# Latent projections of a two-block transformer kernel: from one full-precision product to three rounded ones with ring weights

## What is computed

```python
q = (_rmsnorm(c_q, q_a_g) @ w_uq).reshape(b, n, A_HEADS, A_QK)       # 256 -> 8 * 96
kv = (_rmsnorm(c_kv, kv_a_g) @ w_ukv).reshape(b, n, A_HEADS, A_NOPE + A_V)  # 128 -> 8 * 128
k_nope, v = kv[..., :A_NOPE], kv[..., A_NOPE:]
q, k = _rmsnorm(q, q_norm_g), _rmsnorm(k, k_norm_g)                  # then rope, then attention
```

## Time and profile before

| what | value |
|---|---|
| runs of the kernel before | 891.93 us (891.77 to 892.02) |
| the profiled execution's own time | 892.2 us |
| its span, first to last instruction | 890.4 us |
| PE / PE weight load / DVE / ACT busy | 869.1 / 711.8 / 627.2 / 440.3 us |
| DMA | 136.68 MB, 154 GB/s in the mean |
| granted PE clock, mean | 0.995 of full |

### The profile page before, as it was taken

The page is one execution under the profiler, slowest core; times in us unless marked ns, Lnnn a source line. Parts: engine busy times, 40 slices in busy tenths (PEclk is TensorE's granted clock), DMA queues, the critical chain, the costliest instruction groups (busy, mean ns, idle before and its releaser), DMA issues.

```text
span 890.4 us, 13376 instructions
## 1 busy us (share of the span) xinstructions
PE 869.1 (98%) x5372; PEld 711.8 (80%) x5372; DVE 627.2 (70%) x1252; ACT 440.3 (49%) x750; POOL 21.2 (2%) x16
## 2 busy tenths in 40 slices
PE   7999999999999999999999999999999999999996
PEld 4678477777687777877998888988999888888885
DVE  4532857585826769966699999978588775565666
ACT  3351516544623355655543454466555665555552
POOL 0000000000000000000002212000000000000000
PEclk9999999999999999999999999999999999999998
DMA  9794551100354034303556656441365365545541
GB/s 348 289 329 161 213 189 60 48 25 1 119 220 141 13 130 142 99 10 142 168 190 189 188 186 193 142 144 60 106 200 205 118 204 199 197 172 198 188 167 47
DMA packets 39997, 136.68 MB, mean 154 GB/s; under 512 B 4352, under 2 KB 4480, under 8 KB 39680
## 3 DMA queue, kind: packets, MB, share of 16 engines
q1 hardware_dynamic: 38928, 130.48, 42.9%
q10 hardware_dynamic: 1008, 5.36, 1.6%
HBM read 134.77 MB, written 1.05 MB: 153 GB/s over the span
## 4 chain that ended last, share of the span: by engine, by line
PE 72%; DVE 21%; ACT 3%; DMA 2%; issue 1%; SPq 1%; DVEq 0%; ACTq 0%
PE ps L417 8%; PE ps L973 6%; DVE wlo L1474 5%; PE ps L372 4%; PE ps L373 4%; PE ps L418 4%; DVE AF L1943 4%; PE ps L377 4%; PE ps L735 3%; PE ps L491 2%; PE ps L400 2%; DMA AF<-wmod 2%; PE ps L389 2%; PE ps L462 2%; PE ps L758 2%; PE ps L401 2%
## 5 line engine op out<-in xcount | busy, mean ns | idle before, releaser
L1474 DVE TENSOR_TENSOR wlo<-raw,whi 128x1024 fp32r<-128x1024 f32 (+2 forms) x204 | 231.7, 1158 | 33.4 <-ACT whi L1011 33.2
L1011 ACT ACTIVATE whi<-raw 128x1024 fp32r<-128x1024 f32 (+2 forms) x204 | 203.6, 1005 | 86.5 <-DMA raw<-wpack 45.2
L372 PE MATMUL ps<-hx,whi 128*128 128x256 f32 (+1 forms) x384 | 115.3, 300 | 0.3 <-ACT AF L1352 0.3
L417 PE MATMUL ps<-hx,whi 128*128 128x512 f32 x320 | 113.9, 398 | 0.0
L373 PE MATMUL ps<-hx,whi 128*128 128x256 f32 (+1 forms) x384 | 112.0, 292 | 0.0
L377 PE MATMUL ps<-hx,wlo 128*128 128x256 f32 (+1 forms) x332 | 96.9, 292 | 0.0
L418 PE MATMUL ps<-hx,wlo 128*128 128x256 f32 x320 | 89.8, 281 | 0.0
L372 PEld LDWEIGHTS ps<-hx,whi 128*128 128x128 f32 x384 | 73.4, 191 | 3.8 <-issue 2.3
L373 PEld LDWEIGHTS ps<-hx,whi 128*128 128x128 f32 x384 | 73.5, 191 | 2.0 <-issue 0.7
L462 PE MATMUL ps<-whi,hx 128*128 128x512 f32 (+1 forms) x192 | 71.7, 373 | 0.5 <-ACT acc L1080 0.5
L417 PEld LDWEIGHTS ps<-hx,whi 128*128 128x128 f32 x320 | 60.1, 188 | 14.6
(11 more groups left out here) (293 smaller groups left out, 1666.7 us busy)
## 6 DMA issues: line engine op xcount, KB each, us to landing
raw<-wpack SPq DMA_DIRECT2D x178, 512.0 KB, 4.2
AF<-wmod SPq DMA_DIRECT2D x48, 512.0 KB, 6.1
raw<-wpack SPq DMA_DIRECT2D x24, 256.0 KB, 3.7
XT<-xin SPq DMA_DIRECT2D x4, 512.0 KB, 6.3
raw<-wpack SPq DMA_DIRECT2D x4, 432.0 KB, 4.7
uq<-wuq ACTq DMA_DIRECT2D x2, 768.0 KB, 5.8
cst<-cpack ACTq DMA_DIRECT2D x1, 1093.0 KB, 8.1
AF<-wukv ACTq DMA_DIRECT2D x2, 512.0 KB, 7.1
```

Of the source, the lines that this page charges most:

```text
L372: e.matmul(o, wh[:, b], xh(k), start=j == 0, stop=False, skip_group_check=True)
L417: e.matmul(ps.ap(key, 512).rearrange("p (s n) -> p s n", s=2), wh[:, b], K.hx[:, :, k, 0:256], start=k == 0, stop=False, skip_group_check= ...
L1011: e.activation(W.hi(i), W.raw(i), ACT.Copy).then_inc(*HI.up(j))
L1474: e.tensor_tensor(W.lo(i), W.raw(i), W.hi(i), ALU.subtract).then_inc(*LO.up(j))
```

## The change

The latents are kept as a rounded half and a rest, and `w_uq` and `w_ukv` become chunks in the ring. `kv_proj` and `q_proj` make three fp32r matmuls where they made one f32 matmul. ACT writes the rounded latents where it wrote the plain ones; DVE makes the rests, reading PSUM, ahead of the lows of the `gvkr` chunks, and the banks are free only after that. The `uq` and `wkv` loads leave ACT's queue. In layer 0 `w_ukv` and `w_uq` each pass the ring twice (once for each pair of token tiles), in layer 1 once: three chunks of 1024 and six of 768 columns more, in the order gvkr, ukv, uq, uq, fmix, fgate. The calls of `highs` and `lows` for `gvkr` look one chunk ahead in layer 1 too, and new calls take `uq` (behind the tables) and `ukv` for the second pair. SP's groups of chunks between the modulation pieces are shifted by the new chunks.

```diff
-        def kv_proj(p):
-            pe.wait_ge(K.ukv_in["ukv", l], A[l, "ckv"])
+        def kv_proj(*ps_):
+            c, wh, wl = weights((l, "ukv", ps_[0]), ("w_ukv", l, (0,), ("kvc", 1024)), 1024)
...
+                        pe.wait_ge(A[l, "ckv"], *ps.take((l, nm, t)))
+                        e.matmul(o, K.ckvh[:, x], wh[:, b], start=True, stop=False, skip_group_check=True)
+                        e.matmul(o, K.ckvh[:, x], wl[:, b], start=False, stop=False, skip_group_check=True)
+                        pe.wait_ge(V[l, "ckvl"])
+                        e.matmul(o, K.ckvl[:, x], wh[:, b], start=False, stop=True, skip_group_check=True).then_inc(*M.up((l, nm, t)))
+        def q_proj(p):
+            got = [weights((l, "uq", p, m), ("w_uq", l, (m,), (0, 768)), 768) for m in range(2)]
...
-        kv_proj(0)
         if l == 0:
+            kv_proj(0)
             q_proj(0)
...
-            kv_proj(1)
+            kv_proj(0, 1)
             q_proj(1)
@@ scalar_program @@
-            ps.give(key, A.now())
...
-        e.dma_start(K.uq[:, :], K.wuq[l]).then_inc(*K.uq_in.up(("uq", l)))
-        e.dma_start(g.wkv, K.wukv[l]).then_inc(*K.ukv_in.up(("ukv", l)))
...
         for i in range(3):
-            highs((l, "gvkr", "w", i), NHL - 1 if l else 1)
+            highs((l, "gvkr", "w", i), 1)
+        highs((l, "uq", l, 1), 0)
...
+            highs((l, "ukv", 1), 0)
@@ vector_program @@
+        dv.wait_ge(K.c1["cst"], *bar)
+        for m in range(2):
+            key = (l, "cq", m)
+            dv.wait_ge(A[key])
+            e.scalar_tensor_tensor(out=g.cql[:, m, :], in0=ps.ap(key, N), scalar=C("qag", 2 * l + m, 1), in1=g.cqh[:, m, :], op0=ALU.mult, op1=ALU.subtract).then_inc(*V.up((l, "cql", m)))
+            ps.give(key, A[l, "cqsq", m], V.now())
+        key = (l, "ckv", 0)
+        dv.wait_ge(A[l, "ckv"])
+        e.scalar_tensor_tensor(out=K.ckvl, in0=ps.ap(key), scalar=C("kvag", l, 1), in1=K.ckvh, op0=ALU.mult, op1=ALU.subtract).then_inc(*V.up((l, "ckvl")))
+        ps.give(key, A[l, "ckvsq"], V.now())
         for i in range(3):
-            lows((l, "gvkr", "w", i), NHL - 2 if l else 1)
+            lows((l, "gvkr", "w", i), 1)
...
         V.mark((l, "tab"))
+        lows((l, "uq", l, 1), 0)
         bias(l, 4)
...
             bias(1, 0)
+            lows((l, "ukv", 1), 0)
             kv_take(1, 0, M[l, "kT", 0, 1, 4])
@@ sync_program @@
-    chunks(15, 17)
+    chunks(15, 20)
     mods(2)
-    chunks(17, 18)
+    chunks(20, 21)
     mods(3)
-    chunks(18, 19)
+    chunks(21, 22)
     mods(4)
     mods(5)
     at_out = W.of[0, "wout", 7] + 1
-    chunks(19, at_out)
+    chunks(22, at_out)
```

## The result

The changed kernel takes **918.6 us** in the median of four runs (916.3 to 923.1), the kernel before 891.9 beside it (891.8 to 892.0): 1.031 times the time, with an interval of 1.028 to 1.033. That is 2.6 us over the 916.0 of the forecast and inside its range. The profiled execution took 917.0, its span is 915.2 us. The runs after spread over 7 us, those of before over 0.3.

What follows compares the result with a forecast made beforehand. The order written into the queues, not engine load, was taken to decide, with PE busy 869 of 890 us. A 5.9 + 1.7, kv_proj(1) -0.7, B 4.7 + 0.8, C 10.2 + 1.7 gave +24.3, so 916, range 905 to 923.

Steps and rivals of the forecast that it cites:

- The products: K, V and query projections: 0.68 us per K or V product, 2.1 for 2.6 per query tile; 5.8 less PE work.
- A: Layer 0, fgate 1: its low is made behind the vf copies, so PE starts 5.9 us late, plus 1.7 clock.
- B: Layer 0 loop, step 9: ACT waits for wout 0's load behind gu 0's low; +4.7 us, plus 0.8 clock.
- C: Layer 1: gvkr's banks free 2.7 us late, fgate 0's low behind the normalisations; +10.2 us in all, plus 1.7 clock.
- The loads: Two loads a layer move from ACT's to SP's queue, where waits in order ahead of a load can delay it.
- The clock: Lower clock behind PE's long rests: 1.7 us each at fgate 1 and layer 1's fgate 0, half at step 9.
- The sum: Whole kernel: waits and clock losses less kv_proj(1)'s 0.7 make +24.3 us on the profiled 892.2; median 916.
- the second projections of layer 0: kv_proj(1) in layer 0, where PE is the bound up to the loop: 0.7 us given back.
- My third rival: Worse: each rest costs the clock twice the one row, and gvkr's late start too; 922 to 925, chance 0.10.
- The first rival: Faster: lows are ready at layer 0's fgate 1 and layer 1's fgate 0; all 5.8 us show, 886; chance 0.06.

Runs made afterwards that it cites:

- B undone: Changed kernel with gu 0's low made at step 7 of layer 0's loop instead of step 9 (look-ahead 4 instead of 3): 910.8 us.
- C undone: Changed kernel with layer 1's fgate 0 low made behind the second uq chunk and fgate 1's behind the gate normalisation: 911.2 us.
- the kernel with the filled rest: Changed kernel with twelve matmuls on zeros between the vf products and fgate 1 of layer 0: 914.3 us.
- the last kernel of the experiments: Changed kernel with three calls earlier, layer 1 latents' rests earlier, later layer 1 lows, and fewer ACT roundings at layer 0's Fourier copies and step 9: 892.9 us.
- the kernel with all calls earlier: Changed kernel with lows of layer 0's fgate 1 and gu 0, layer 1's fgate 0 and 1, and layer 1's latents' rests made earlier: 894.4 us.

## Why the prediction was right

**The products** were as forecast: 0.70 us for 0.68, 4.2 for 4.2.

**A**: forecast 5.9 us late and 1.7 for the clock, 7.6. The trace has 6.0 and 2.6. The kernel before with only this low moved measured 8.0 (6.0 late in its trace, 1.2 for the clock), the changed kernel with it moved back 10.1. The wait was right; the clock's 1.7 lies between what single executions show, 1.1 to 2.6. That the two measured numbers differ by 2 us is left open: the median of the changed kernel, from four runs over 7 us, is in one of them alone.

**B**: forecast +5.2, less 0.5, and 0.8 for the clock. The trace shows 5.5 and some 1.7 for the clock (0.57 over 8 us, half of them at rest), and undoing it gave 7.8. The place (step 9), the cause (wout 0's load behind gu 0's low) and ACT's wait (4.5 us, in the 4 to 6 foreseen) hold. Later in the loop 1.2 us came back where I had put 0.5, so 6.0 is left where 5.5 were forecast. In the profiled execution with B undone the shift still grows by 1.1 at this place, so the undoing is worth 5 us there; the 7.8 between the medians holds other things too (1.3 us of A's clock among them, and the changed kernel's spread).

**C**: forecast +10.2 and 1.7 for the clock, from one chain through gvkr's banks and fgate 0's low. The trace shows fgate 0 12.2 us later than its surroundings, PE resting 9.5. The two parts, undone one by one, gave 7.4 and 4.6, which is 12.0 for 11.9. Gvkr was 2.8 late for 2.7. What I left to a rival was its clock: the rest of 3.3 us did lower it (0.72 over 6 us, 1.7 lost), and that makes most of the difference between 12.2 and 10.2.

**The loads.** The Trainium skill, "Trainium Kernel Development and Optimization", section "Key Constraints", says that issuing from several queues only saves issue time, and I had set B against that. The two don't meet: wout 0 was on SP's queue before the change too, and its load waited for its raw slot, which gu 0's low frees. Making that low two steps earlier, with every load left on its queue, took B away. No run puts the loads of `uq` and `wkv` back on ACT's queue, so nothing here shows what that move costs, for or against that statement. **The clock.** By the Trainium skill, "TensorE: Matmul & The Clock Gate", section "What's actually happening", the throttled state is the default, so all three rests should be followed by a fall. The trace agrees, and has one behind gvkr's rest as well; of the twelve others of over 5 us that I read in six more kernels none is without a fall. Behind a rest of 3.3 us the clock stayed at 1.00 in one kernel of six.

**The sum.** +24.3 was forecast, the profiled execution has +24.8 on the span, and 1.6 us of it are missing only because the clock kept up at the start; the median is +26.7. The term that was mis-sized is the clock: 4.2 in the sum, against 2.6 and 1.7 behind A and B, 1.7 behind gvkr and 1.7 behind fgate 0 (0.50 from 364.2 to 365 and 0.56 over 3 us), together 7.7. Not all of that reaches the end: 1.2 us came back behind B and near 1 behind fgate 0. Rests of 0.3 and 0.4 us that the kernel before has in these places are gone, which is a part of it. By the shifts the terms are A 6.0 and 2.6, the second projections of layer 0 -1.1 (0.7 forecast), B 6.0, C 12.2 with gvkr's clock in it, and 0.7 from there to the end: 26.4, which is 24.8 and the 1.6. My third rival, the clock twice each and gvkr too, gave 922 to 925 and was nearer the truth in its mechanism than the forecast; the median lies between. **The first rival**, that the covers hold and 5.8 us show, falls twice: the covers don't hold, and with them restored by hand the time is 893 to 897, not 886. I had taken it that a microsecond off PE shows once PE waits for nobody. The runs say that DVE, with 13 us more of its own work, then becomes the late one in layer 1, and ACT with its rounding in layer 0.

## What to carry to other kernels

When a change puts new entries into a ring that is served by calls in a fixed order, list for every old entry at which call it was made and at which it will be made now; three calls that came too late cost 22 us here (undone together), for 5.8 us of saved matmuls. A look-ahead can be repaired in one line at each place, but the extra work on the helper engine stays and can eat the gain. A call moved later to relieve one wait makes the next one: look where its work lands. And check both signs: work added to the bounding engine can show for the most part where work removed from it does not.

## What the runs showed of the hardware that I had not expected

A rest of TensorE is dearer than its length. All rests of 5.4 to 9.5 us that I read, fifteen in seven kernels, were followed by the lower clock; behind A it cost 1.1 to 2.6 us. The rest of 3.3 us ahead of gvkr was, in five kernels of six; the clock by windows of the sixth, the one with C undone, stays at 1.00 from 320 to 338. The rest of 1.7 us ahead of the vf products, which ten of the kernels have, was followed by it in one:

```profile
102.00:104.00 2.00, 0.33 (x1) 0.33 (x2) 1.79 (x7) 2.00 (x4) 0.00 (x0) 0.97 0.71 176
104.00:106.00 2.00, 2.00 (x3) 0.70 (x3) 1.86 (x5) 0.10 (x1) 0.00 (x0) 0.50 0.97 385
```

These are windows of the kernel with the filled rest, where the vf products took 8.8 us instead of 7.1. In the last kernel of the experiments a rest of 1.95 us in the loop was followed by nearly 7 us at the lower clock, while a rest of 2.6 us ahead of the first modulation product, near 10 us in the kernel with all calls earlier, was followed by none. So the length of a short rest alone does not tell whether the clock falls, and at one place it differs from one execution to the next, as does the fall behind the one-column matmuls near 83 us (0.51 in the profiled execution of before, 1.00 in that of after). Twelve matmuls on zeros inside a long rest kept the clock up. The changed kernel spread over 7 us in four runs and the one before over 0.3 beside it; but before spread over 4 us in 21 later runs, and the kernel with all calls earlier over 5.6 in 12. The mean granted clock of the changed kernel's four runs goes with their time: 0.985, 0.981, 0.977 and 0.974 for 916.3, 917.0, 920.2 and 923.1 us. That the clock makes the spread is likely; it was not tried.
